# First layer's opening: scale and shift loaded by column halves, four input chunks started before the second halves arrive

## The reference, cut to what matters

```python
silu_c = jax.nn.silu(c);  silu_cc = jax.nn.silu(c_ctx)
sh1, sc1, g1, sh2, sc2, g2 = jnp.split(silu_c @ w_mod[l] + b_mod[l], 6, axis=-1)
csh1, csc1, ...            = jnp.split(silu_cc @ w_mod[l] + b_mod[l], 6, axis=-1)
hx = modulate(rmsnorm(x_lat, norm1_g[l]), sh1[:, None], sc1[:, None])   # h * (1 + scale) + shift
hc = modulate(rmsnorm(x_ctx, norm1_g[l]), csh1, csc1)
dk, dv, nk, nv, dq, nq, pz, su, sv, gz = split_cols(hx @ w_in, COL_SIZES)
```

## Time and profile before

| | us |
|---|---|
| median of the runs | 2014.68 |
| the profiled execution | 2014.5 |
| its span | 2012.7 |
| PE busy | 1846.0 (92%) |
| DVE / ACT / POOL busy | 823.4 / 442.1 / 122.1 |
| mean granted clock | 0.982 |

### The profile page before, as it was taken

The page is one execution under the profiler, slowest core; times in us unless marked ns, Lnnn a source line. Parts: engine busy times, 40 slices in busy tenths (PEclk is TensorE's granted clock), DMA queues, the critical chain, the costliest instruction groups (busy, mean ns, idle before and its releaser), DMA issues.

```text
span 2012.7 us, 26909 instructions
## 1 busy us (share of the span) xinstructions
PE 1846.0 (92%) x11196; PEld 1096.5 (54%) x11196; DVE 823.4 (41%) x1249; ACT 442.1 (22%) x774; POOL 122.1 (6%) x135
## 2 busy tenths in 40 slices
PE   7999999999999998999888899999999988888786
PEld 4887766677888433333223488877896222222222
DVE  3686555665854322222212466667655010101001
ACT  3212244443222200000000332244443000000000
POOL 1080200000000000000000041200000000000000
PEclk9999999999999999999999999999999999999999
DMA  8545411113647899999999656633578999999997
GB/s 331 189 127 159 154 48 64 53 59 108 207 152 279 349 413 427 429 429 428 428 429 429 256 176 221 215 121 105 173 281 330 385 429 426 429 427 429 428 428 292
DMA packets 78798, 565.55 MB, mean 281 GB/s; under 512 B 8856, under 2 KB 9008, under 8 KB 53616
## 3 DMA queue, kind: packets, MB, share of 16 engines
q1 hardware_dynamic: 77648, 557.72, 70.3%
q0 software_dynamic: 512, 4.40, 0.6%
q10 hardware_dynamic: 544, 2.10, 0.3%
HBM read 563.11 MB, written 1.07 MB: 280 GB/s over the span
## 4 chain that ended last, share of the span: by engine, by line
PE 64%; DMA 25%; DVE 7%; issue 2%; ACT 1%; SPq 1%; POOL 0%; DVEq 0%; ACTq 0%
PE PS L941 41%; PE PS L1439 17%; DMA e_h<-in_moe_w 16%; DMA arena<-in_moe_w 9%; PE PS L1176 1%; PE PS L1382 1%; DVE nab L1967 1%; PE PS L1198 1%; DVE wr L1948 1%; PE PS L996 1%; DMA ring_par<-in_w_mod 1%; SPq L863 0%; ACT wr L1520 0%; PE PS L1026 0%; DVE small L2242 0%
## 5 line engine op out<-in xcount | busy, mean ns | idle before, releaser
L941 PE MATMUL PS<-hTr,wr 128*128 128x512 f32 (+1 forms) x2688 | 518.2, 349 | 4.6 <-DVE hTr L2035 2.8
L941 PEld LDWEIGHTS PS<-hTr,wr 128*128 128x128 f32 x2688 | 428.4, 190 | 72.0 <-issue 10.2
L1439 PE MATMUL PS<-e_h,arena 128*32 128x512 f32 x1312 | 268.4, 614 | 36.5 <-DMA arena<-in_moe_w 19.0
L1439 PE MATMUL PS<-arena 128*32 128x512 f32 x1216 | 262.7, 611 | 28.7 <-DMA arena<-in_moe_w 25.4
L1948 DVE TENSOR_TENSOR wr<-ring_par,wr 128x1024 fp32r<-128x1024 f32 x150 | 188.8, 1259 | 157.0 <-ACT wr L1520 156.4
L1520 ACT ACTIVATE wr<-ring_par 128x1024 fp32r<-128x1024 f32 x151 | 159.5, 1056 | 306.7 <-PE PS L941 284.1
L1439 PE MATMUL PS<-arena,nab 128*32 128x512 f32 x1088 | 201.3, 601 | 11.3 <-DMA arena<-in_moe_w 10.7
L941 PE MATMUL PS<-wr,hTr 128*128 128x512 f32 x816 | 190.7, 393 | 4.0 <-DVE wr L1948 4.0
L2457 DVE TENSOR_TENSOR x_work<-x_work,PS 128x512 f32<-128x512 f32 x72 | 45.8, 684 | 339.8 <-PE PS L941 339.8
L941 PEld LDWEIGHTS PS<-wr,hTr 128*128 128x128 f32 x816 | 152.9, 189 | 38.3 <-DVE wr L1948 5.8
L1439 PEld LDWEIGHTS PS<-e_h,arena 128*32 128x32 f32 x1312 | 73.3, 113 | 170.3 <-issue 156.1
(11 more groups left out here) (217 smaller groups left out, 1768.4 us busy)
## 6 DMA issues: line engine op xcount, KB each, us to landing
arena<-in_moe_w SPq DMA_DIRECT2D x90, 2048.0 KB, 17.2
e_h<-in_moe_w SPq DMA_DIRECT2D x58, 2048.0 KB, 17.7
ring_par<-in_w_in SPq DMA_DIRECT2D x136, 512.0 KB, 3.7
e_wr<-in_moe_w SPq DMA_DIRECT2D x30, 2048.0 KB, 17.4
ring_par<-in_w_mod SPq DMA_DIRECT2D x92, 512.0 KB, 4.2
ring_par<-in_w_br SPq DMA_DIRECT2D x64, 256.0 KB, 3.3
ring_par<-in_w_out SPq DMA_DIRECT2D x16, 512.0 KB, 3.6
ring_par<-in_moe_w SPq DMA_DIRECT2D x4, 2048.0 KB, 12.6
```

The lines of the kernel that those rows point to most:

```text
L941: return nc.tensor.matmul(o, a, b, start=first, stop=last)
L1439: ins = nc.tensor.matmul(PS[r:r + CAP, bank + h, :], src[:, k, r:r + CAP], space[:, kk * D + h * 512:kk * D + (h + 1) * 512], start=(k == ...
```

## The change

The loads change their cut. An item of scale or shift now holds two row parts (2 kp and 2 kp + 1) of only 512 columns: items 0 to 3 are the scale's first 512 columns, 4 to 7 the shift's; items 10 to 13 and 14 to 17 are the second 512 columns. Items 8 and 9 are the first halves (k = 0 to 3) of the weights of chunks 0, 1 and of 2, 3, items 18 and 19 the second halves. Scale and shift get separate banks (6 and 3). Everything behind them (copy, turning, `modA`, `modB`, modulation, rounding) is done once for each half, and the four first chunks do their products with k = 0 to 3 between the matmuls of the second halves of scale and shift. POOL subtracts for all four. Per-load contiguous pieces go from 4 KB to 2 KB in these 20 items.

```diff
+OPEN, OPEN_BANKS, OPEN_MODS = 4, (0, 4, 1, 5), (6, 3)
...
-        for n in range(MOD0):
-            for k in range(KD):
-                mod_item(0, n, k)
+        HALF_MODS = MOD0 * KD // 2
...
+        open_mods(0)
+        open_weights(0)
+        open_mods(1)
+        open_weights(1)
...
+                    if kind == "open_mod":
+                        half, part, kp = idx // HALF_MODS, 1 - idx % HALF_MODS // 4, idx % 4
+                        dst = dst.rearrange("p (k n) -> p k n", k=2)
+                        c = part * D + half * 512
+                        src = w_mod_v[0, :, 2 * kp:2 * kp + 2, c:c + 512]
...
-            for k in range(1, KD):
-                keep_warm(2, 5)
-                mod_chunk(0, 1, k)
+            def open_mod(i):
+
+
+                half, n, kp = i // HALF_MODS, i % HALF_MODS // 4, i % 4
+                w = take(("open_mod", 0, i)).rearrange("p (k n) -> p k n", k=2)
+                for kk in range(2):
+                    k = 2 * kp + kk
+                    for jj in range(2):
+                        j = 2 * half + jj
+                        o = PS[32 * j:32 * j + 32, OPEN_MODS[n], 0:MQ]
+                        ins = nc.tensor.matmul(o, cond[:, k, :], w[:, kk, jj * MQ:(jj + 1) * MQ], start=(k == 0),
+                                               stop=(k == KD - 1), tile_position=(0, 32 * j), skip_group_check=True)
+                ins.then_inc(mod_step.sem, 1)
...
+            def open_chunk(c, kp):
+
+
+                half = kp // 2
+                pe.wait_ge(*w_lo.at(0, 2 * half + c // 2 + 1))
+                pe.wait_ge(*h_lo.at(0, 2 * kp + 2))
+                for k in (2 * kp, 2 * kp + 1):
+                    cols_ = slice(512 * (c // 2) + k % 4 * 128, 512 * (c // 2) + (k % 4 + 1) * 128)
+                    i = three(PS[:, OPEN_BANKS[c], :], wr[:, c % 2, 0, cols_], wr[:, c % 2, 1, cols_],
+                              hTr[:, 0, k, :], hTr[:, 1, k, :], k == 0, k == KD - 1, False)
+                if kp == 3:
+                    i.then_inc(chunk_sum.sem, 1)
+                elif kp == 1 and c % 2:
+                    i.then_inc(open_sum, 1)
+
+            for i in range(HALF_MODS):
+                if i > 3:
+                    keep_warm(2, 2)
+                open_mod(i)
+                if 3 <= i <= 6:
+                    transposes(0, tr_banks(0)[i - 3:i - 2])
+                if i == 5:
+                    open_post(0, 0)
+            open_post(0, 1)
+            pe.wait_ge(*tmp_act.at(0, 1))
+            keep_warm(8, 2)
+            for i in (0, 1, 2):
+                open_mod(HALF_MODS + i)
+                keep_warm(2, 2)
+            open_chunk(0, 0)
+            open_mod(HALF_MODS + 3)
+            open_chunk(1, 0)
+            transposes(0, tr_banks(0)[4:5])
+            open_mod(HALF_MODS + 4)
+            open_chunk(0, 1)
+            open_post(1, 0)
+            open_mod(HALF_MODS + 5)
+            open_chunk(1, 1)
+            open_mod(HALF_MODS + 6)
+            open_mod(HALF_MODS + 7)
+            transposes(0, tr_banks(0)[5:6])
+            open_chunk(2, 0)
+            open_post(1, 1)
+            transposes(0, tr_banks(0)[6:7])
+            open_chunk(2, 1)
             pe.wait_ge(*mod_ready.at(0, 1))
+            transposes(0, tr_banks(0)[7:])
+            open_chunk(3, 0)
+            open_chunk(3, 1)
+            for c, kp in ((0, 2), (1, 2), (0, 3), (1, 3), (2, 2), (2, 3), (3, 2), (3, 3)):
+                open_chunk(c, kp)
...
+            def open_high(i):
+
+
+                slot, use = item_at["open_w", 0, i]
+                act.wait_ge(loaded[slot], 16 * (use + 1))
+                if i > 1:
+                    act.wait_ge(open_sum, i - 1)
+                nc.scalar.activation(wr[:, :, 0, i % 2 * 512:i % 2 * 512 + 512],
+                                     ring[:, slot, :].rearrange("p (q n) -> p q n", q=2), ACT.Copy).then_inc(w_hi.sem, 1)
```

More of the change, by code:

```diff
@@ L680, in summed_items, with open_mods, open_weights @@
                 item("mod", l, KD * (first_summed(l) + a) + k, mod_taken.at(l, KD * a + k + 1))
-        for n in range(MOD0):
-            for k in range(KD):
-                mod_item(0, n, k)
+        HALF_MODS = MOD0 * KD // 2
+        def open_mods(half):
+            for n in range(HALF_MODS):
+                item("open_mod", 0, half * HALF_MODS + n, mod_step.at(0, half * HALF_MODS + n + 1))
+        def open_weights(half):
+            for pair in range(OPEN // 2):
+                item("open_w", 0, 2 * half + pair, w_lo.at(0, 2 * half + pair + 1))
+        open_mods(0)
+        open_weights(0)
+        open_mods(1)
+        open_weights(1)
+        opened = len(items)
         for l in range(L):
             for q in range(NW + 2):
-                item("chunk", l, q, w_lo.at(l, q + 1))
+                if l or q >= OPEN:
+                    item("chunk", l, q, w_lo.at(l, q + 1))
                 summed_items(l, BY_Q[l].get(q - 2, ()))
@@ L718, in mod_pairs @@
             order = tr_banks(l)
+            if l == 0:
+                return [(s, kp, order.index((s, kp))) for kp in range(4) for s in range(2)]
             if l:
                 return [(s, kp, n) for n, (s, kp) in enumerate(order)]
-            return [(s, kp, order.index((s, kp))) for kp in range(4) for s in range(2)]
         def mod_bank(l, n):
@@ new lines, in open_post @@
+            def open_post(half, n):
+                if half == 0:
+                    pe.wait_ge(open_part, n + 1)
+                else:
+                    pe.wait_ge(*mod_part.at(0, n + 1))
+                col = 256 + 16 * (1 - n)
+                rows = slice(64 * half, 64 * half + 64)
+                turned = PS[:, 7, col:col + 16].rearrange("p (j c s) -> p c j s", j=PQ, c=2)[:, :, 2 * half:2 * half + 2, :]
+                for c in range(2):
+                    i = mm(turned[:, c, :, :], modp[rows, n, c * 128:(c + 1) * 128],
+                           cst[rows, C_SELC + 4 * half:C_SELC + 4 * half + 4], True, True)
+                i.then_inc(open_cols, 1)
@@ L1562, in modulate @@
             def modulate(l, upto):
+                if l == 0:
+                    for half in range(2):
+                        open_high(2 * half)
+                        if half == 0:
+                            open_high(1)
+                            act.wait_ge(open_ready, 1)
+                        else:
+                            act.wait_ge(*mod_ready.at(*MODULATED[l]))
+                        for t in (4 * half, 4 * half + 2):
+                            part_modulated(l, t)
+                            part_high(l, t)
+                            part_high(l, t + 1)
+                    open_high(3)
+                    return
                 act.wait_ge(*mod_ready.at(*MODULATED[l]))
@@ L1863, in _ @@
                     roots(2 * l, 0, 1)
[L1864 to L1873, removed]
+                    for i in range(OPEN):
+                        slot, _ = item_at["open_w", 0, i]
+                        cols_ = slice(i % 2 * 512, i % 2 * 512 + 512)
+                        pool.wait_ge(*w_hi.at(0, i + 1))
+                        pool.tensor_tensor(wr[:, :, 1, cols_], ring[:, slot, :].rearrange("p (q n) -> p q n", q=2),
+                                           wr[:, :, 0, cols_].bitcast(f32), ALU.subtract).then_inc(w_lo.sem, 1)
                 else:
```

134 lines of the change are left out of this document (63 added, 71 removed).

## The result

| | before | after |
|---|---|---|
| median of 16 runs each, us | 2013.78 (2012.64 to 2015.38) | 2018.07 (2016.31 to 2019.77) |
| the profiled execution, us | 2014.5 | 2018.22 |
| its span, us | 2012.7 | 2016.4 |
| first matmul of the sv parts, us | 61.97 | 66.83 |

The changed kernel is slower: 1.0021 times the time of before, 95% interval 1.0015 to 1.0028, 4.3 us. The forecast was 2018.7 us, on the line of 0.2%; the interval has that line inside, so on which side of it the kernel lies is not settled.

The account below looks back on a forecast made before the run. PE was taken as the bound, so the end moves with the start of the sv parts: 61.97 to 66.1 us, 4.1 us later. Added to 2014.5 us this gave 2018.6, forecast 2018.7 us; eight-in-ten range 2015.3 to 2021.2 us.

Parts of the forecast that it names:

- The term that decides: Scale or shift item on PE: two column groups instead of four raise it from 0.57 to 1.01 us.
- PE as the bound of the second half: From 30.7 us PE has no wait; its work sums to 35.40 us and ends at 66.1 us.
- the sum: PE's work added up from profile rows through both halves; sv parts begin at 66.1 us, 4.1 us later than before.
- The start: First four items on PE, gapless from 10.88 us: upper clock level at 15.0 us, fourth item ends at 16.84 us.
- the first half behind it: PE after the first four items: four items, transposes, fillers and a turning, together 9.37 us, to 26.2 us.
- the gap: Between the halves: PE's wait ends at 28.8 us, then eight fillers of 1.9 us, to 30.7 us.
- the second rival: Clock rises late or falls in the gap between halves: 2.05 us on top, 2020.7 us; chance 0.15.
- Side by side after all: Rival: PE takes an item's four matmuls on two groups in 0.57 us; 2013.5 us, not slower; chance 0.13.
- Loads and tokens as the bound: Rival: a load, subtraction or the second half's tokens hold up PE; 1 to 4 us, 2021 us; chance 0.04.
- the 396 of the estimate: Loads of halved pieces: 396 GB/s, 1.32 us an item instead of 1.28, costed at nothing.
- The tokens' thin cover: Second half's tokens ready at 54.8 us, the block needing them starts at about 55.3: cover of 0.4 us.

Follow-up runs that it names:

- twice_before: Kernel before, with the four matmuls of each of the sixteen scale and shift items issued twice, the first set unread: 2016.71 us, ratio 1.0018.
- four_groups: Changed kernel with its half columns cut in four quarters of 128 instead of two of 256, so all four column groups work: 2012.59 us, ratio 0.9994.
- early_fillers: Changed kernel using four column groups, gap fillers ahead of the wait, no pair fillers in the second half, thirteen fillers before the first item: 2010.36 us, ratio 0.9984.

## Why the prediction came true, point by point

- **The term that decides was right.** An item costs 0.99 us, forecast 1.01; the experts of layers 0 and 1 had shown it. twice_before and four_groups show it from both sides. The forecast counted records of 256 columns, where the number of records and of columns says the same; four_groups shows that it is the columns.
- **PE as the bound of the second half was right.** From 32.52 us to 66.83 us are 34.3 us; the sum without its first item was 34.4. The first 128x512 matmul comes at 36.24 us, forecast 35.7.
- **The start was right, too:** four items took 5.89 us (5.96 in the sum) because work without gaps brought the upper clock level earlier; before, it came at 18.7. twice_before shows the same with the old loads: its first four items, without a gap too, are done at 16.66 us. The fit is in part luck, since items that follow each other directly cost less than the price taken (1.86 us for two, from 46.52 to 48.38 us).
- **Mis-sized: the first half behind it.** The last item ends near 25.4, not 26.2 us. The first four are done 0.3 us sooner than in the sum. Three times a group of transposes and its fillers cost 0.49 and 0.54 us (16.55, 17.04, 17.58) instead of 0.58 and 0.64, together 0.6 us: there is no change of tiles between the two, and I had priced each as if it stood between items. The gap behind it was right, 2.57 us against 2.6.
- **Mis-sized the other way: the gap.** The sum had full speed behind it. The clock fell, as the second rival had it; fillers and the first item cost 2.80 + 1.78 = 4.58 us instead of 1.9 + 1.01, 1.7 us more (rival: 2.05). I gave that rival 0.15, on the strength of one pause of 1.21 us without a fall, while the new one was twice as long. That was the weak step: the rival was part of what happened, and the start of the second half was hit (30.74 us after the fillers, forecast 30.7) because 0.9 us too much in the first half stood against 0.9 us too little in the fillers. The first item added 0.8 us more.
- **Side by side after all** is refuted, by every row of an item.
- **Loads and tokens as the bound** did not come up in the changed kernel. DMA ran at 381 to 390 GB/s from 10 to 25 us, under the 396 of the estimate, and it was covered. The tokens' thin cover held: the last four `part_low` run from 54.30 us, and no block waits for them.
- **How much of the hit is luck.** The forecast of 2018.7 us was 0.6 us above the median. Its difference was 4.1 us; sv moved by 4.9, the spans by 3.7 and the medians by 4.3 us. The fall of the clock at 155 us, which only the profile of before has, makes the step from 4.9 to 3.6 us. The forecast also stood on a median of three runs, 2014.68 us; sixteen give 2013.78. So mechanism and size of the deciding term were right, and the last microsecond is errors that cancel.

## What to carry to other kernels

When a loop over narrow tiles is cut anew, count the columns that each column group gets, not the matmuls or their records: halving the width that is at hand halves the groups unless it is divided over all of them again. A pause of PE between phases can cost twice, once itself and once at half clock behind it. It did so between 24 and 28 us in two kernels, and not everywhere, so look at windows of 1 us behind each pause. Where it does, fillers belong into the pause, ahead of the wait, and not behind it. And where PE is the only bound over the whole rest of the kernel, one moment early on (here: when sv starts) predicts the median time to about a microsecond; a single execution can lie some 3 us from it.

## What the runs showed of the hardware that was not expected

- Pauses of 2.5 us with a short turning in them (changed kernel) and of 2.35 us behind one (four_groups) were followed by 3.4 us at half clock in the windows; a pause of 1.21 us was not the earlier trace rows, and neither was one of 2.50 us ahead of 160.21 us in the changed kernel. In early_fillers pauses of 2.36, 0.71 and 0.70 us in a row, with items of 0.65 us between, were followed by a fall as well.
- A column group takes time by the columns that it gets: 512 in 0.57 us, as two records of 256 or four of 128, and 1024 in 0.99 us, whether two groups work or four.
- A two-input subtraction of DVE (128x512) takes 0.68 us alone (2.49 us for four) and 1.2 to 2.4 us beside POOL: 2.65 us for a pair in the kernel before, 2.41 us for one in early_fillers. In the kernel before, this cost some 1.9 us on the path to the first blocks; twice_before got it back by accident.
- Pieces of 2 KB instead of 4 KB go with a lower DMA rate of the full queue, about 387 GB/s (10 to 25 us) instead of 411; twice_before, with the old pieces, has 406 to 411. It mattered only once PE had been made fast enough to wait for it.
